# Attention heads in pairs on array halves, bias rows by one skewed DMA: a one-core hybrid encoder layer on Trainium2

## What is computed

```python
aq, ak, av, iq, ik, iw, gq, gk, gv, gz, gb, ga = split(h @ w_in)
# sparse attention: 8 heads, 4 key heads, head size 64
score  = sum over index heads of iw * relu(iq . ik)      # picks the top keys
logits = q . k_sel / 8 + rel_bias[rel_bucket(key - query)]
p      = softmax(where(valid, logits, -inf)); attn = p @ v_sel
# gated delta rule: 4 heads of 128, chunks of 64 tokens, a state from chunk to chunk
sol = solve_triangular(I + tril(kb k^T * decay), [v*beta, kb*exp(gc)])
o   = q exp(gc) S + (tril(q k^T) * decay) v_new;  S = S exp(g_last) + k^T v_new
o   = rms_norm(o, gnorm_w) * silu(gz)
mixed = concat(attn, o) @ w_out
```

## Time and profile before

| | us |
|---|---|
| median of 3 runs | 1691.98 |
| lowest and highest | 1685.35, 1698.99 |
| the profiled execution | 1694.69 |
| its span | 1693.0 |
| granted TensorE clock, mean over the span | 0.964 |

### The profile page before, as it was taken

One profiled execution on the slowest core, in us unless ns is written; L12 is line 12 of the kernel. 1 busy time (PEld: TensorE's weight loads), 2 busy tenths in 40 slices (PEclk: granted clock), 3 DMA queues, 4 the chain that ended last, 5 costly groups with the idle time before them and its releaser, 6 DMA issues. The chain is left out here.

```text
span 1693.0 us, 29486 instructions
## 1 busy us (share of the span) xinstructions
PE 1551.3 (92%) x11820; PEld 1434.3 (85%) x11826; DVE 688.0 (41%) x1283; ACT 530.3 (31%) x908; POOL 133.5 (8%) x172
## 2 busy tenths in 40 slices
PE   5899999999999699989978998769799999999996
PEld 2899999999998699978956666559799999999996
DVE  3522322223224525886664443343522332233233
ACT  3533112221222424342244344442533112211233
POOL 2200000000002400000021002102200000000000
PEclk9999999999999899999999898979899999999998
DMA  8535335435224132122030101133122222222221
GB/s 307 171 119 164 119 120 161 124 100 184 68 63 142 35 90 79 50 55 63 1 107 15 51 3 42 53 94 87 45 68 83 66 75 74 74 75 75 68 67 64
DMA packets 203930, 148.31 MB, mean 88 GB/s; under 512 B 17307, under 2 KB 189876, under 8 KB 203832
## 3 DMA queue, kind: packets, MB, share of 16 engines
q1 hardware_dynamic: 190584, 99.92, 20.6%
q0 software_dynamic: 13248, 47.00, 8.0%
HBM read 139.98 MB, written 6.64 MB: 87 GB/s over the span
## 5 line engine op out<-in xcount | busy, mean ns | idle before, releaser
L2445 PE MATMUL pair<-h_hi,w_hi 128*128 128x320 f32 x1888 | 436.0, 312 | 3.1 <-ACTq L2199 2.3
L2445 PE MATMUL pair<-h_lo,w_hi 128*128 128x320 f32 x1888 | 431.7, 310 | 0.0
L2445 PE MATMUL pair<-h_hi,w_lo 128*128 128x320 f32 x1888 | 431.3, 310 | 0.0
L280 DVE TENSOR_TENSOR w_lo<-w_raw,w_hi 128x1024 fp32r<-128x1024 f32 x174 | 213.1, 1226 | 327.5 <-ACT w_hi L275 315.3
L2445 PEld LDWEIGHTS pair<-h_hi,w_hi 128*128 128x128 f32 x1888 | 315.4, 188 | 16.7 <-issue 12.7
L2445 PEld LDWEIGHTS pair<-h_lo,w_hi 128*128 128x128 f32 x1888 | 316.8, 188 | 0.0
L2445 PEld LDWEIGHTS pair<-h_hi,w_lo 128*128 128x128 f32 x1888 | 316.4, 188 | 0.0
L275 ACT ACTIVATE w_hi<-w_raw 128x1024 fp32r<-128x1024 f32 x174 | 182.8, 1054 | 302.3 <-PE pair L2445 180.6
L407 DVE SCALAR_TENSOR_TENSOR x_t<-pair,gate,x_t 128x320 f32 (+1 forms) x112 | 49.0, 479 | 220.2 <-PE pair L2445 154.5
L2445 PE MATMUL pair<-a_hi,w_hi 128*128 128x320 f32 x528 | 121.8, 312 | 2.2 <-DVEq L417 2.2
L2445 PE MATMUL pair<-a_hi,w_lo 128*128 128x320 f32 x528 | 120.3, 309 | 0.0
(11 more groups left out here) (364 smaller groups left out, 1734.8 us busy)
## 6 DMA issues: line engine op xcount, KB each, us to landing
w_mod_raw<-w_mod POOLq DMA_DIRECT2D x28, 1024.0 KB, 7.9
w_raw<-ffn_w_gate SPq DMA_DIRECT2D x44, 512.0 KB, 3.8
w_raw<-ffn_w_up SPq DMA_DIRECT2D x44, 512.0 KB, 3.9
w_raw<-ffn_w_down SPq DMA_DIRECT2D x32, 512.0 KB, 4.1
w_raw<-w_in SPq DMA_DIRECT2D x24, 512.0 KB, 3.7
w_raw<-ffn_w_down SPq DMA_DIRECT2D x16, 384.0 KB, 3.4
w_mod_a<-w_mod POOLq DMA_DIRECT2D x4, 1024.0 KB, 10.8
w_mod_b<-w_mod POOLq DMA_DIRECT2D x4, 1024.0 KB, 24.2
```

The source lines that it names most:

```text
L280: dve.tensor_tensor(w_lo[:, u % HL], w_raw[:, u % RAW], w_hi[:, u % HL].bitcast(F32), ALU.subtract).then_inc(lo_done, 1)
L2445: mm = pe.matmul(pair[u % 2][0:width, b, 0:HALF], w[:, 0:width], x_parts[part][:, k, b * HALF:(b + 1) * HALF], start=(k == 0 and v == 0), ...
```

## The change

1. **Bias rows.** SP sends the table once, ahead of the weights of in-projection unit 6, as 8 x 128 rows of 640 into a buffer in memory whose row pitch is 641 within a head. Read back with a pitch of 640, each row starts one element earlier: the rows come finished and in order. 8 plain loads bring them to rel8 when the in-projection's loads are through and the mask is made; POOL brings the samples' version by 2 loads. The flip matmuls, the ACT copies and POOL's small write go.
2. **Pairs.** A job of the prompt is two heads whose keys stand on the two halves of the partitions: 16 pair jobs and 8 sample jobs, 24 slots. The whole chain of a job now lies within its slot: logits at the start, `biased` (DVE), `exps` (ACT), `normed` (DVE, scaling included), `turn` and `turned`; the values follow in the next slot. For t < 2 both heads are turned and copied in one. `level` holds one slot.
3. **Samples.** A sample's own keys stand as 16 columns between two windows of 16 (304 columns), so that their turned weights fall on rows where v_tok has its values; the copies v_last go. POOL makes q_z for all samples once.
4. **Order at the ends.** Unit ("ak", 1) is last of the in-projection, behind the four gz; the square root and exponentials stand ahead of its evacuation. The prompt's part of h_hi and h_lo is made in the slots (`mixed_prompts`). w_hi of the first w_out unit is made between o_square(3) and old_part(4).
5. **w_out.** Five loads for each unit put the attention rows in the order of the pairs. `project_mixed` does the first two units for tokens 0 to 319 first, and then for the others with k = 4 to 7 ahead of k = 0 to 3.

```diff
-            + [("ak", i) for i in range(2)] + [("gz", i) for i in range(GH)])
+            + [("ak", 0)] + [("gz", i) for i in range(GH)] + [("ak", 1)])
 def mix_loads(sp):
+                if v == 6:
+                    sp.wait_ge(S["tbl"], 2)
+                    sp.dma_start(bass.AP(skewed.tensor, skewed.offset, [[P * (REL + 1), AH], [REL + 1, P], [1, REL]]),
+                                 tbl[0:AH].unsqueeze(1).broadcast_to([AH, P, REL])).then_inc(S["tbl_out"], 16)
...
+            sp.wait_ge(S["mask"], 5)
...
+            for k in range(4):
+                for s in range(2):
+                    h = head_of(k, s)
+                    sp.dma_start(rel8[:, h], bass.AP(skewed.tensor, skewed.offset + h * P * (REL + 1) + P - 1, [[REL, P], [1, SEQ]]))\
+                        .then_inc(S[f"rel_in{k}"], 16)
             sp.wait_ge(unit_done, U_OUT + 1)
-            load_flipped(0)
-            load_flipped(1)
...
+                for s in range(2):
+                    for pr in range(2):
+                        sp.dma_start(w_raw[s * AD:(s + 1) * AD, u % RAW, 2 * pr:2 * pr + 2], wo_att[s, :, pr, :, cols]).then_inc(S["raw_extra"], 16)
+                sp.dma_start(w_raw[:, u % RAW, 4:KD], wo[:, 4:KD, cols]).then_inc(raw_in[u % RAW], 16)
 def mix_pool(pool):
-            pool.dma_start(a["_table"], tbl[0:AH, :]).then_inc(S["tbl_out"], 16)
...
+            pool.memset(q_z[:], 0.0).then_inc(S["qz"], 1)
+            pool.wait_ge(S["qz"], 2)
+            for g_ in range(AKV):
+                rows = slice(AD * (g_ % 2), AD * (g_ % 2) + AD)
+                pool.tensor_copy(q_z[rows, :, g_].rearrange("p b (r t) -> p r b t", r=2),
+                                 aq_t[rows, 2 * (g_ // 2):2 * (g_ // 2) + 2, SEQ:].rearrange("p r (b t) -> p r b t", b=NB)).then_inc(S["qz"], 1)
 def delta_act(act, exps, turned, values_out, keys_ready, ends):
+            def beside(part=None, after=None):
+                j = next(jobs)
+                if j >= N_PAIRS and j + 1 < N_JOBS:
+                    keys_ready(j + 1 - N_PAIRS)
+                exps(j)
+                if part:
+                    part()
+                turned(j, 0)
+                if after:
+                    after()
+                turned(j, 1)
...
             o_square(3)
+            act.wait_ge(S["kb_turned"], NB)
+            wait_extra(act, U_OUT)
+            split_hi(act, U_OUT)
             old_part(4)
-            jobs(1)
+            beside()
             o_square(4)
             o_stds(1)
 def attention_pe(pe):
+            def logits(j):
+                n = keys_of(j)
...
+                for s in range(2):
+                    pe.matmul(pair[0][:, s, 0:n], ident_bf[:], mask_bf[:, MASK_AT[t]:MASK_AT[t] + n], start=True, stop=False)
+                for s in range(2):
+                    rows = slice(AD * s, AD * s + AD)
+                    mm = pe.matmul(pair[0][:, s, 0:n], aq_t[rows, k, cols_of(t)], ak_t[rows, k // 2, 0:n], start=False, stop=True)
+                mm.then_inc(S["logits"], 1)
...
                     for k in range(t + 1):
-                        mm = pe.matmul(pair[1][AD * r:AD * r + AD, 1, g_ * P:(g_ + 1) * P], v_tok[:, k, g_ * AD:(g_ + 1) * AD],
-                                       pt_sb[:, j % 2, k * P:(k + 1) * P], start=(k == 0), stop=(k == t))
+                        for s in range(2):
+                            g_ = 2 * (k4 // 2) + s
+                            mm = pe.matmul(pair[1][AD * s:AD * s + AD, 1, k4 * P:(k4 + 1) * P], v_tok[:, k, g_ * AD:(g_ + 1) * AD],
+                                           pt_sb[:, s, k * P:(k + 1) * P], start=(k == 0), stop=(k == t), skip_group_check=True)
```

## The result

The changed kernel takes 1713.36 us (median of 4 runs, 1712.22 to 1714.46), the kernel before 1691.76 in the same measurement: ratio 1.0112, 95% interval 1.0079 to 1.0145. It is slower by 1.1%, where 1690.0 and a small gain were forecast. The profiled execution has a span of 1710.5, 17.5 more than before.

What follows compares the result with a forecast made beforehand. TensorE, busy 1551.3 of 1693.0 us, was taken as the bound; stage -28 and bias transfer +26 gave -2, so 1692.7 profiled and 1690.0 as median. The forecast's own range was 1675 to 1712, with rivals 1652 to 1722.

Steps and rivals of the forecast that it cites:

- D: In-projection: duration of the skewed bias transfer ahead of unit 6's weights, taken as 38 us (9 to 64), costing +26.
- nothing is lost up to 14 us: In-projection: slack for the skewed transfer before TensorE must wait for unit 3's evacuation, about 14 us.
- Flipped rows: Stage of delta rule and attention: 8 turning matmuls and 8 ACT copies go, -8.5 us (0 to -9).
- Logits: Stage, prompt's heads: a pair on two row halves overlaps for a quarter of 23.5 us, -5.9 (0 to -11.8).
- values: Stage: both heads' matmuls alternate between column halves and run beside each other, -9.8 us (0 to -12).
- model of neighbours: Stage, logits of a pair: in order A A B B only A's second and B's first record meet, a quarter.
- Samples: Stage, sample jobs: POOL makes all queries once, so TensorE's wait for DVE's copies goes, -11.4 us (or -6).
- Start: Head of the stage: last in-projection unit evacuated after square root and exponentials, -1.6 of 3.1 us idle.
- Tail: End of the stage: w_out prepared and started earlier, despite ACT waiting for its weights, -7 of 34.88 us (0 to -12).
- Given back: Stage: each slot holds a job's whole chain, shortfall averaging 1 us in 16 slots, +16 (+5 to +32).
- the hidden transfer: Rival, in-projection: D is 14 us or less, so the bias transfer is hidden; 1664 us, chance 0.3.
- the slow one: Rival, in-projection: D is 64 us, price 50, and the stage gains only 12; 1730 us, chance 0.1.

Runs made afterwards that it cites:

- b_half: Kernel before plus half the skewed transfer's rows (1.31 MB, same 8 partitions), which nothing reads: 1707.41 us, measured once.
- b_skew8: Kernel before plus the skewed transfer alone, out of 8 partitions on SP's queue, nothing reading it: 1734.86 against 1695.37 us, ratio 1.0238.
- b_rows: Kernel before with finished bias rows alone, skewed from a table in memory, no flip matmuls or copies: 1698.73 against 1696.50 us, ratio 1.0016.
- a_serial: Changed kernel, skewed transfer reading memory, a pair's values one head after the other: 1671.58 us, ratio 0.9874 to the kernel before.
- a_qz: Changed kernel, skewed transfer reading memory, queries copied by DVE in each sample job: 1679.16 us, ratio 0.9919 to the kernel before.
- a_exps: Changed kernel, skewed transfer reading memory, square root and exponentials behind the last in-projection evacuation: 1673.18 us, ratio 0.9869 to the kernel before.
- a_dram_late: Changed kernel, skewed transfer reading memory, first w_out split moved behind the last job: 1662.57 us, ratio 0.9813 to the kernel before.

## Why the prediction was right and wrong

The step that failed is the size of one term: the duration D of the skewed transfer. I took 38 us, between two readings of the small write (35 and 42); the landing of unit 6 at 654.5 after that of unit 5 at 600.7 gives about 52 (53.8 less the 2 for its own load). The rest of that step held: nothing is lost up to 14 us (`b_half`: 13), the wait goes through ACT's order and the PSUM pair, TensorE comes back at half the clock. With D = 52 the forecast's own working gives 38 + 2 = 40 in the place of 26, and `b_skew8` measured 39.5. The error was one of method: the time of eight lone packets was taken for the pace of a stream. Alone a packet took 0.275 us of an engine; in the stream, at 50 GB/s and a share of 0.48, it is 0.39 (an estimate from the windows: 7.7 engines busy for 19.5 packets a microsecond). The Trainium skill, page "SBUF — State Buffer", section "Door 1: The DMA port swizzle", led to an estimate of 48 us and a cost near 36; the forecast named it and passed over it. By that the sum would have been 1700.

That term is not the whole difference of 23.4 us between 1690.0 and 1713.4. The forecast for the profiled execution was 1692.7, and it took 1712.2, 19.5 more: about 14 from D, 4.5 from the rest of the in-projection, which the sum did not have (3.7 of it the later stretch at a granted clock of 0.80), 1.7 from the stage, and 0.9 less in the first units of w_out. The other 3.8 between the two differences lie in which execution was profiled: before it stood 2.7 above the median, after 1.1 below.

The stage was forecast at 245 and took 246.7. Term by term:

- Flipped rows: -8.5 forecast, nothing found (`b_rows`). A busy line was counted as path though the forecast itself said that this stretch alternates with DVE and ACT; the lower clock of the stretch was not in the forecast at all.
- Logits -5.9 and values -9.8 forecast; their lines fell by 11.1 and 13.5. The model of neighbours was too strict (`a_serial`, and the rows of the logits). If these lines count in full, their 8.9 us beyond the forecast make up for the flipped rows, which would be luck; no run takes the pairs alone, so it is not shown.
- Samples -11.4: 10.6 by `a_qz`.
- Start -1.6: a wait of 2.6 comes back in `a_exps`, the stage with it 2.4 longer.
- Tail -7: from the end of the last state step on DVE to the first w_out matmul it was 34.9 (the window from 1088.90 in the earlier trace rows) and is 28.4 (1113.69 to 1142.05), so -6.5. The wait that the forecast named on ACT is there with 11.3 us and cost 6 to 9 (`a_dram_late`).
- Given back +16: TensorE's idle time in the stage is 58.2 where it was 54.0, although 11.4 + 1.6 of waits went; so about 17 of new ones came. The groups put 25.3 before the samples' turns (10.5 of it in the tail), where 0.5 stood, while the wait for the scaling before the prompt's turns stayed as it was, 13.2 before and 12.8 now: the chain in the slot shows in the sample jobs and not, as forecast, in the 16 of the prompt. So the size came out right by luck, at another place.

The rivals: the hidden transfer is refuted (D was not 14), the slow one had the right side with 50 for D = 64. The forecast left the 2 us of the slow restart out of the rivals: by its own working D = 64 costs 52, and the points at which the kernel is slower by 1% lie at D = 57 and 41, not 59 and 43. Both sides of the sum were named; the sign was decided by 14 us of one transfer.

## What to carry to other kernels

Before a transfer is put ahead of weights, count which partitions it reads: here copies of eight rows in neighbouring partitions came at some 50 GB/s, on SP's queue and on POOL's, and the weights behind them waited. Write the few rows out once and copy from memory (195 GB/s), or lay them four partitions apart (193). And a busy line of one engine is not a gain when it goes, as long as nobody has looked at what else fills the stretch and at the clock that it runs on.

Do not let an engine with the critical chain behind it wait for a load that can only start when the chain's last store is done: split those weights one step later.

## What the runs showed of the hardware

Eight source rows in partitions 0 to 7: 49 to 51 GB/s at a mean share of the 16 engines of about 0.48; in partitions 0, 4, to 28, or in memory: 193 to 195 GB/s at 0.52. Weights on another queue, issued 0.9 us behind the slow transfer, landed only near its end, 54.7 us after their issue. Two heads' values on the two column halves take 1.09 us when they alternate and 1.58 when they follow each other, where one head alone took 1.09; two heads' logits on the two row halves take 1.13 one behind the other, where one took 1.12. And the granted clock over the same piece of the stage stood at 1.00 in five kernels that leave it as it was, 0.89 without the flip matmuls, and 0.78 to 0.83 with the change.
